# Two of a trunk's eight gate chunks issued inside the first attention steps, and one linear-attention tile per gate half

## The reference

```python
(aq, ak, av, ag, iq, ik, iw, bq, bk, bv, bg, blr) = split(rmsnorm(x) @ even_w_in)
a_out = dsa_attention(aq, ak, av, iq, ik, iw, rel_bias) * silu(ag)   # 8 heads of 64
g_out = head_rmsnorm(gla_chunked(bq, bk, bv, log_a)) * silu(bg)      # 4 heads, values of 128
mix = concatenate([a_out, g_out]) @ even_w_out
```

## Time and profile before

| | us |
|---|---|
| median of 3 runs (lowest to highest) | 1117.87 (1117.31 to 1119.39) |
| profiled execution | 1114.39 |
| its span, first to last instruction | 1112.6 |
| gate loop on PE, 16 halves | about 286 to 422 |
| the search on DVE | about 163 to 432 |
| first pair's steps 0 to 7 | 435 to 512 |
| mean granted clock of PE (1 is 2.4 GHz) | 0.961 |

### The profile page before, as it was taken

The page is one execution under the profiler, slowest core; times in us unless marked ns, Lnnn a source line. Parts: engine busy times, 40 slices in busy tenths (PEclk is TensorE's granted clock), DMA queues, the critical chain, the costliest instruction groups (busy, mean ns, idle before and its releaser), DMA issues.

```text
span 1112.6 us, 14632 instructions
## 1 busy us (share of the span) xinstructions
PE 1011.4 (91%) x5642; PEld 815.4 (73%) x5642; DVE 689.8 (62%) x1220; ACT 458.0 (41%) x780; POOL 268.1 (24%) x199
## 2 busy tenths in 40 slices
PE   4996889989999999789999778989999999895997
PEld 3885679968877776557777566878788888684885
DVE  5314679997779597874554462574539393967042
ACT  6323552253422323335555563433246363573031
POOL 2210212102332322313131564120313122124000
PEclk8998999989999999899999898999999999997999
DMA  7251102101112223101010434322211121112052
GB/s 242 63 71 38 39 1 77 39 1 38 57 56 87 76 67 114 40 25 43 16 53 24 156 106 154 111 75 76 81 52 57 38 57 39 38 38 92 22 189 75
DMA packets 71738, 75.81 MB, mean 68 GB/s; under 512 B 5064, under 2 KB 58360, under 8 KB 71672
## 3 DMA queue, kind: packets, MB, share of 16 engines
q1 hardware_dynamic: 70400, 73.30, 21.1%
q10 hardware_dynamic: 1272, 1.62, 1.3%
HBM read 58.13 MB, written 16.25 MB: 67 GB/s over the span
## 4 chain that ended last, share of the span: by engine, by line
PE 76%; DVE 13%; ACT 5%; issue 4%; POOL 1%; DMA 1%; DVEq 0%; SPq 0%; POOLq 0%; ACTq 0%
PE ps L1588 21%; PE ps L1590 20%; PE ps L1589 20%; PE ps L1833 2%; PE ps L1817 2%; PE ps L1676 2%; PE ps L1768 1%; DVE prob L1370 1%; PE ps L1678 1%; PE ps L1765 1%; PE ps L1677 1%; ACT relu L861 1%; DVE ysL L1525 1%; PE ps L1736 1%; DVE y L1517 1%
## 5 line engine op out<-in xcount | busy, mean ns | idle before, releaser
L1588 PE MATMUL ps<-hH,wH 128*128 128x512 f32 x384 | 159.1, 414 | 15.5 <-DVE qkL L1358 10.0
L1228 DVE TENSOR_SCALAR_CACHE_REDUCE junk<-score,cand 128x384 bf16<-128x384 f32 (+2 forms) x192 | 169.7, 942 | 1.3
L1590 PE MATMUL ps<-hH,wL 128*128 128x512 f32 x384 | 152.7, 398 | 0.0
L1589 PE MATMUL ps<-hL,wH 128*128 128x512 f32 x384 | 152.3, 397 | 0.0
L612 POOL TENSOR_TENSOR wL<-raw,wH 128x1024 fp32r<-128x1024 f32 x32 | 77.1, 2413 | 157.3 <-ACT wH L768 157.3
L1588 PE MATMUL ps<-h1H,w_slot_H 128*128 128x512 f32 x256 | 100.4, 392 | 2.5 <-DVE h1L L1472 2.5
L1590 PE MATMUL ps<-h1H,w_slot_L 128*128 128x512 f32 x256 | 100.3, 392 | 0.0
L1589 PE MATMUL ps<-h1L,w_slot_H 128*128 128x512 f32 x256 | 100.2, 391 | 0.0
L1588 PEld LDWEIGHTS ps<-hH,wH 128*128 128x128 f32 x384 | 73.6, 192 | 35.3 <-issue 21.3
L1590 PEld LDWEIGHTS ps<-hH,wL 128*128 128x128 f32 x384 | 73.6, 192 | 16.2
L1589 PEld LDWEIGHTS ps<-hL,wH 128*128 128x128 f32 x384 | 73.9, 192 | 13.3
(11 more groups left out here) (242 smaller groups left out, 2266.7 us busy)
## 6 DMA issues: line engine op xcount, KB each, us to landing
raw<-in_even_w_in SPq DMA_DIRECT2D x32, 512.0 KB, 4.0
xt<-in_x SPq DMA_DIRECT2D x16, 512.0 KB, 5.6
raw<-in_odd_w_in SPq DMA_DIRECT2D x16, 512.0 KB, 3.9
gate_d<-gst SPq DMA_DIRECT2D x16, 256.0 KB, 2.2
raw_row<-in_even_w_out SPq DMA_DIRECT2D x8, 512.0 KB, 3.4
x_d<-xt SPq DMA_DIRECT2D x8, 512.0 KB, 2.6
raw_row<-in_odd_w_out SPq DMA_DIRECT2D x8, 512.0 KB, 3.2
xt<-x_d SPq DMA_DIRECT2D x8, 512.0 KB, 4.7
```

Of the source, the lines that this page charges most:

```text
L1228: return steps(dve.tensor_scalar(junk1[:, j % 3, 0:(qb + 1) * P], score_of(qb), threshold, None, op, ALU.add, accum_out=dst[:, j:j + 1]))
L1588: pe.matmul(dst, lH, rH, start=k == 0, stop=False)
L1589: pe.matmul(dst, lH, rL, start=False, stop=False)
L1590: return pe.matmul(dst, lL, rH, start=False, stop=k == nk - 1)
```

## The change

- Chunks 22 and 23 become pair 0's query and key; `bg`'s last two gate chunks become 24 and 25 (`C_LATE`). The gate loop has 12 halves in place of 16.
- The four late gate halves are units among the fillers, behind (0, 2) and (0, 3). `FILLERS` has six parts in each of steps 0 to 3 and four in steps 4 to 7 (before: 4, 4, 2, 2, 2, 2, 4, 4). The first six units go round over banks 3, 5 and 0, and PE waits for the bank's last user. Banks 3 and 5 are also used by the logits from step 4 on, so `head_logits(4)` waits until the gate halves are copied.
- ACT evicts a late gate half (`late_gate`: copy, wait for POOL's last product, sigmoid) at the start of the step behind the one in which it ends; POOL multiplies it behind `near_bias` and `near_first`; SP stores it. `high` and `low` of each chunk from 24 on stand a step behind the last unit of the chunk two before.
- `gla_at` puts one tile in each half: turn, update, output of tile t at halves `8t//7 + 1`, `+2`, `+3` (before `7t//4 + 1`, `+2`, `+4`). DVE's `gla_step(t)` stands at pass `35 + 5t//2` (before `34 + 3t`). The store of a tile is issued one half behind its output.

```diff
...
-    C_AV, C_BV, C_BQK, C_AG, C_BG, C_PAIR, C_WOE, C_ODD, C_WOO = 4, 8, 12, 16, 20, 24, 32, 40, 56
+    C_AV, C_BV, C_BQK, C_AG, C_BG, C_PAIR, C_LATE, C_WOE, C_ODD, C_WOO = 4, 8, 12, 16, 20, 22, 24, 32, 40, 56
+    EARLY_G = C_PAIR - C_AG
...
-    PRODUCTS += [("pair", p, f) for p in range(PAIRS) for f in range(4)]
+    PRODUCTS += [("pair", 0, f) for f in range(2)]
+    UNITS = [("pair", 0, 2), ("pair", 0, 3)]
+    UNITS += [("g", c, hf) for c in (C_LATE, C_LATE + 1) for hf in range(2)]
+    UNITS += [("pair", p, f) for p in range(1, PAIRS) for f in range(4)]
+    PRODUCTS += UNITS
...
-        turned = 7 * t // 4 + 1
-        return turned, turned + 1, min(turned + 3, 15)
+        turned = 8 * t // 7 + 1
+        return turned, turned + 1, turned + 2
...
+    def unit_bank(unit):
+
+        if unit in UNITS[:6]:
+            return (3, 5, 0)[UNITS.index(unit) % 3]
+        return 7 if unit == ("pair", 0, 1) else 0
+
+    def before_in_bank(unit):
+
+        for other in PRODUCTS[nth_product(*unit) - 1:nth_product("pair", 0, 0) - 1:-1]:
+            if unit_bank(other) == unit_bank(unit):
+                return other
...
-    parts = [(p, f, part) for p in range(PAIRS) for f in range(4) for part in range(4)][8:]
+    parts = [(unit, part) for unit in UNITS for part in range(4)]
     FILLERS, ended = [], {}
-    for a, count in enumerate([4, 4, 2, 2, 2, 2, 4, 4] + [2] * 16):
+    for a, count in enumerate([6] * 4 + [4] * 4 + [2] * 16):
         FILLERS.append(parts[:count])
-        for p, f, part in parts[:count]:
-            ended[p, f] = a
+        for unit, part in parts[:count]:
+            ended[unit] = a
...
+        for t in range(NT):
+            if gla_at(t)[2] + 1 >= 2 * EARLY_G:
+                store_gla(t)
...
+        def store_late_gate(n, hf):
+            sp.wait_ge(silu_done, 2 * (EARLY_G + n) + hf + 1)
+            sp.dma_start(gate_d[EARLY_G + n, :, hf * HALF:(hf + 1) * HALF], gst_late[:, hf, :]).then_inc(gate_out[hf], 16)
...
-        load_raw(C_PAIR + 3)
+        load_raw(C_LATE + 1)
...
+        for n in range(2):
+            load_raw(pair_chunk(1, n))
+            for hf in range(2):
+                store_late_gate(n, hf)
+        load_raw(pair_chunk(2, 0))
+        load_raw(pair_chunk(2, 1))
...
-        for i in range(KD):
+        for i in range(EARLY_G):
...
+            for n in range(2):
+                for hf in range(2):
+                    if a == ended["g", C_LATE + n, hf] + 1:
+                        pool.wait_ge(proj_copied, copy_count("g", C_LATE + n, hf))
+                        pool.tensor_tensor(gst_late[:, hf, :], gst_late[:, hf, :], g_sig_late[:, :], ALU.mult).then_inc(silu_done, 1)
+            for c in range(C_LATE, C_WOE):
+                if a == ended[last_unit(c - 2)] + 1:
+                    low(c)
...
+        def late_gate(n, hf):
+
+            act.wait_ge(proj_full, nth_product("g", C_LATE + n, hf) + 1)
+            if n:
+                act.wait_ge(gate_out[hf], 16 * (EARLY_G + n))
+            bank = unit_bank(("g", C_LATE + n, hf))
+            act.activation(gst_late[:, hf, :], ps[:, bank, :], ACT.Copy)
+            act.wait_ge(silu_done, 2 * (EARLY_G + n) + hf)
+            act.activation(g_sig_late[:, :], ps[:, bank, :], ACT.Sigmoid).then_inc(proj_copied, 1)
...
-            for p, f in ended:
-                if ended[p, f] == a - 1:
-                    split_pair(p, f)
+            for kind, x, f in UNITS:
+                if ended[kind, x, f] == a - 1:
+                    if kind == "pair":
+                        split_pair(x, f)
+                    else:
+                        late_gate(x - C_LATE, f)
...
+            for c in range(C_LATE, C_WOE):
+                if a == ended[last_unit(c - 2)] + 1:
+                    high(c)
...
-                if n == 34 + 3 * t:
+                if n == 35 + 5 * t // 2:
...
+            kind, x, f = unit
+            hf, j = divmod(f, 2) if kind == "pair" else (f, x % 2)
             if part == 0:
-                pe.wait_ge(w_lo, C_PAIR + 2 * p + j + 1)
-                if (p, f) == (0, 0):
+                pe.wait_ge(w_lo, (pair_chunk(x, j) if kind == "pair" else x) + 1)
+                before = before_in_bank(unit)
+                if unit == ("pair", 0, 0):
                     pe.wait_ge(proj_copied, copy_count("g", C_PAIR - 1, 1))
-                elif (p, f) == (0, 1):
+                elif unit == ("pair", 0, 1):
                     pe.wait_ge(st_ready, NCH - 2)
-                else:
-                    pe.wait_ge(proj_free, low_count("pair", p, f) - 1)
-            last = weights_first(PAIR_BANK(p, f), (wH[:, j], wL[:, j]), hf, ks=range(2 * part, 2 * part + 2))
+                elif before is not None and before[0] == "pair":
+                    pe.wait_ge(proj_free, low_count(*before))
+                elif before is not None:
+                    pe.wait_ge(proj_copied, copy_count(*before))
...
+            if n == NT // 2:
+                pe.wait_ge(proj_copied, copy_count("g", C_LATE + 1, 0))
...
```

More of the change, by code:

```diff
@@ L296, in last_product, with last_unit, pair_chunk @@
             return nth_product("bqk", BQK_ORDER[c - C_BQK], 1)
[L297 to L299 removed]
+        return nth_product(*last_unit(c))
+    def last_unit(c):
+        if c < C_PAIR or C_LATE <= c < C_LATE + 2:
+            return ("g", c, 1)
+        return ("pair", 0 if c < C_LATE else (c - C_LATE) // 2, 2 + c % 2)
+    def pair_chunk(p, j):
+        return (C_LATE + 2 * p if p else C_PAIR) + j
     def before_in_slot(c):
@@ L484, in _ @@
                 sp.dma_start(gate_d[c - C_AG, :, hf * HALF:(hf + 1) * HALF], gst[:, hf, :]).then_inc(gate_out[hf], 16)
-                if hf == 0 and c >= C_AG + 3:
-                    store_gla(c - C_AG - 3)
+                for t in range(NT):
+                    if 2 * (c - C_AG) + hf == gla_at(t)[2] + 1:
+                        store_gla(t)
             load_raw(c + 3)
-        for t in range(5, NT):
-            store_gla(t)
+        for t in range(NT):
+            if gla_at(t)[2] + 1 >= 2 * EARLY_G:
+                store_gla(t)
+        def store_late_gate(n, hf):
+            sp.wait_ge(silu_done, 2 * (EARLY_G + n) + hf + 1)
+            sp.dma_start(gate_d[EARLY_G + n, :, hf * HALF:(hf + 1) * HALF], gst_late[:, hf, :]).then_inc(gate_out[hf], 16)
         def load_near(p):
@@ L711, in _ @@
                     scale_gla(2 * (a - 26) + t)
-            for p in range(1, PAIRS):
-                for j in range(2):
-                    if a == ended[p - 1, 2 + j] + 1:
-                        low(C_PAIR + 2 * p + j)
+            for n in range(2):
+                for hf in range(2):
+                    if a == ended["g", C_LATE + n, hf] + 1:
[4 more added lines that the diff above has]
+                    low(c)
             if 25 <= a < 33:
@@ L936, in gla_result @@
             ins.then_inc(o_out, 1)
-        for i in range(16):
+        for i in range(2 * EARLY_G):
             c, hf = C_AG + i // 2, i % 2
@@ L998, in _ @@
                     exponent(a, i)
-            for p in range(1, PAIRS):
-                for j in range(2):
-                    if a == ended[p - 1, 2 + j] + 1:
-                        high(C_PAIR + 2 * p + j)
+            for c in range(C_LATE, C_WOE):
+                if a == ended[last_unit(c - 2)] + 1:
+                    high(c)
             if a == 30:
@@ L1413, in _ @@
                 for hf in range(2):
+                    dve.wait_ge(gate_out[hf], 16 * EARLY_G)
+            if a == NT + 2:
+                for hf in range(2):
                     dve.wait_ge(gate_out[hf], 16 * KD)
@@ L1420, in _ @@
                 gate_b(pieces_at(a - 1)[1])
-            for p, f in ended:
-                if ended[p, f] == a - 1:
+            for kind, p, f in UNITS:
+                if kind == "pair" and ended[kind, p, f] == a - 1:
                     low_pair_result(p, f)
@@ L1850, in _ @@
             for part in range(4):
-                pair_part(0, f, part)
+                unit_part(("pair", 0, f), part)
         pe.wait_ge(o_out, NT)
@@ L1860, in _ @@
                 if parts:
-                    pair_part(*parts.pop(0))
+                    unit_part(*parts.pop(0))
                 if i == 0:
@@ L1867, in _ @@
             for part in parts:
-                pair_part(*part)
+                unit_part(*part)
             if pieces_at(a)[1] is not None:
```

26 lines of the change are left out of this document (14 added, 12 removed).

## The result

| | before | after |
|---|---|---|
| median, us (lowest to highest, runs) | 1117.59 (1116.26 to 1119.39, 4) | 1147.16 (1145.75 to 1148.70, 4) |
| ratio to before (95% interval) | | 1.0271 [1.0253, 1.0289] |
| profiled execution, its span | 1114.39, 1112.6 | 1145.75, 1144.0 |
| mean granted clock of PE | 0.961 | 0.942 |

The change makes the kernel 2.7% slower: 29.6 us by the medians, 31.4 by the spans. The forecast was 23.5.

The account below looks back on a forecast made before the run. It took the PE-DVE hand-over of tiles, not PE's load, to set the gate loop's length. First logits 8.5 us later plus steps 15.0 us longer gave 23.5, so 1141 us, range 1124 to 1153.

Parts of the forecast that it names:

- rival (3): Gate loop: the clock stays low through the alternating tiles, up to 23 us in five tiles; 1155 us; chance 12%.
- alternation in the loop: Gate loop: PE and DVE wait for each other in turn for tiles 1 to 5; search ends 7.7 us later.
- low clock in the loop: Gate loop: PE's five pauses slow the matmuls behind them, 0.5 us a tile, 2.5 in all; bounds nothing to 14.
- shorter hand-over: From search end to first logits: 1.3 us in place of 2.97, as DVE no longer waits for the second unit.
- steps 0 to 7, without low clock: First pair's attention steps: more PE work and new waits, 87.9 us against 72.9 by the same arithmetic, 15.0 longer.
- low clock in the steps, beyond before's 4.1: Steps 0 to 7: the 4.1 us of low clock in before carried over unchanged, giving 92.0 against 77.0.
- upper bound, +20: Steps 0 to 7: 20 us longer if PE's idle 7 us before step 0 put it at the low clock.
- Rival (2): Steps 0 to 7: masks cover the extra work, only the loop costs, 8.5 plus 0 to 3; 1128 us; chance 12%.
- Rival (1): Gate loop: PE sets the pace, DVE's `att` copy being there at each next turn; 21.8 us less; 1110; chance 9%.
- The table loads: Steps 2 and 4: ACT's late sigmoid needs a 1.28 us load, the next exponential another; no added drain counted.
- step 4's wait for POOL's product: Step 4: the late gate waits for POOL's product, which stands behind `near_bias`; PE waits 3.5 us.
- DVE's collisions with POOL: Steps 1 to 4: POOL's conversions beside mask making cost DVE 2.1 us each, nothing while PE is late; uncovered up to 8.

Follow-up runs that it names:

- experiment 2: The changed kernel with useless matmuls filling PE's five pauses ahead of the attention products of tiles 2 to 6; 1137.53 us, 1.0182.
- experiment 9: The changed kernel with 40 useless matmuls in PE's 9.48 us pause ahead of the first logits; 1144.58 us, 1.0252.
- experiment 1: The changed kernel with PE's tile stages in each gate half ordered output, update, turn in place of turn, update, output; 1120.89 us, 1.0040.
- experiment 4: The changed kernel with the four late gate halves' sigmoid computed as an exponential, so no function table is switched; 1147.91 us, 1.0278.
- experiment 8: On top of experiment 1, POOL's product of a late gate half moved ahead of `near_bias`; 1122.23 us, 1.0051.
- experiment 6: On top of experiment 5, `high` and `low` of chunk 24 ahead of step 0, fillers respread to 6, then 4 a step; 1113.86 us, 0.9972.
- experiment 5: On top of experiment 1, the six filler parts of step 0 issued ahead of the first logits; 1116.82 us, 1.0008.

## Why the prediction was right, and which terms were mis-sized

The forecast was slower by 23.5 us, 1141; it is 29.6, 1147.16, inside the range and nearly midway to rival (3) at 1155. The spans, term by term (31.4 in all):

| term | forecast | measured | from |
|---|---|---|---|
| alternation in the loop | +7.7 | +7.5 | experiment 2 |
| low clock in the loop | +2.5 | +10.1 | after against experiment 2 |
| shorter hand-over | -1.7 | -1.5 | 1.64 us for 3.18, `need` to first logits |
| ahead of the loop | 0 | -2.2 | first turn at 294.76 for 296.98 |
| steps 0 to 7, without low clock (87.9 for 72.9) | +15.0 | some +15 | see below |
| low clock in the steps, beyond before's 4.1 | 0 | some +4 | experiment 9, step 1, step 4 |
| behind step 8 | 0 | -1.4 | 599.4 for 600.8 us |

**The mechanism was right.** PE and DVE hand each tile to and fro, and the search ends later with fewer halves beside it. Experiment 1 shows that it is the order, by taking the alternation away with all halves where they were. Stepping both streams gave 7.7 us; the chip gave 7.5.

**The low clock in the loop was mis-sized by four.** The step that failed was "I take 0.5 a tile": it gave each pause about what one pause in before's steps had cost. In after the low level lasts for three stretches of 13.65 us in the loop, where before has none there. And what runs in them right behind the pause is turn, update and output, which DVE waits for: some 4 us more in each of three tiles and nothing in the other two (experiment 2), not 0.5 in each of five. The upper bound of that term, 14, was for 1.5 times the time in every tile; 10.1 lies near it. Rival (3), 1155, had the right mechanism and was too large: it is 14 us above the forecast, where the result is 6. The argument against it, matmuls between the pauses, was no protection. It also shows in the pauses: the five took 3.3, 3.6, 0.8, 5.1 and 0.7 us, 13.4 in all where 18.5 was forecast, as slower gate halves used up the rest.

**The steps.** Steps 2, 3, 5, 6 and 7 came within 0.5 us of the working without low clock, and step 0 too where the clock was held up (8.9, experiment 9). The excess over that working is 8.15 us: 2.5 in step 0, shown to be the clock; 1.65 in step 1 and 3.0 in step 4 (granted clock of that step 0.78), which I put down to it as well, but from the rows alone; and 1.0 in small sums. For step 4 two other traces speak too: in experiments 4 and 9 its wait is as long but its granted clock is 0.88, and it lasts 14.6 us in place of 15.4. To carry over before's 4.1 us was the mistake; 8.15 is about twice that. The forecast had the case in its upper bound, +20 with the pause ahead of step 0; the steps are at +19.1. `wL` of chunk 24 came 6.73 us after step 1's start (forecast 6.8), and PE's waits were 2.28, 1.16 and 3.95 us (2.7, 1.5, 3.5).

**Some of the closeness is luck.** The two clock terms were some 12 us too small together. The -2.2 ahead of the loop and the -1.4 behind step 8, neither of them forecast, took 3.6 of that away.

**Rival (2), the steps' work covered:** false, +19.1. **Rival (1), PE paces the loop:** false for this order. But its condition is what experiment 1 brings about, and there the loop gains 8.7 us, not 21.8: PE has time to spare then (its pause of 9.48 us), and the search with 12.7 us of waits left sets the end.

**The table loads.** The forecast had the loads themselves in steps 2 and 4. Leaving them out gave 1.0 us in step 2 and nothing in PE's wait of step 4 (experiment 4), and changes the ratio by 0.0007, inside both intervals. The drain was left at nothing, and rightly. The Trainium skill ("ScalarE: Activation LUTs", "What ACT_TABLE_LOAD costs") adds some 1.38 us of drain to a switch. The trace does not agree: the sigmoid starts 1.29 us behind the load's start, and from the gate's copy to ACT's next copy it is 2.39 us in after and 1.09 without the switch, 1.30 in all. **Half right:** step 4's wait for POOL's product. It is there with its size, but experiment 8 shows that without it the masks take its place, so that of the 3.95 us it costs under 2 (steps 4 and 5 together, 25.3 for 23.6). The forecast's sum by steps could not show that, since it went from PE's waits and not from what is late behind them. And DVE's collisions with POOL, taken as hidden under PE, are so in after: DVE is busy 63.46 us in the steps where it was 55.17, and PE waits nowhere for a mask.

```profile
448.50:544.60 96.10, 88.24 (x487) 66.49 (x487) 63.46 (x112) 41.11 (x76) 31.88 (x31) 0.92 0.15 42
```

Experiment 6 shows them again as soon as PE is earlier.

The -2.2 ahead of the loop and -1.4 behind step 8 are within the scatter of single executions, as far as the traces show. The first turn starts at 294.76 and 294.83 in after and experiment 9 and at 296.30 in experiment 4, with the same instructions ahead of it. Behind step 8, experiments 1 and 4 have 599.2 and 601.5 us, with the same work there. What makes this scatter is open.

## What to carry to other kernels

Before taking work off the fuller engine, step both streams through the hand-overs: where each instruction in a cycle waits for the other engine's last, that cycle sets the time, and freed time becomes pauses. In such a cycle, what the other engine waits for goes first and what waits for it goes last; here this one line was worth 26 of 30 us, while in the kernel before, where it put one awaited stage behind another, it cost 4. A pause of TensorE ahead of a short chain that somebody waits for cost more here than its own length, through the clock: filling pauses with useless matmuls is a cheap way to measure how much, and moving real work into them (experiments 5 and 6) is what turned the change into a small gain. But work that is taken out of a step can open new pauses there, and then the low clock only moves on (experiment 5).

## What the runs showed of the hardware

Five pauses of PE of 0.7 to 5.1 us, 16 to 21 us apart, left the granted clock at 0.81 over 90 us (0.98 with them filled, 1.00 in experiment 1, where one of 1.6 us is left), though PE was busy 88% of that time. The three of 3.3, 3.6 and 5.1 us each have a stretch of 13.65 us at the lower level with them, the two of 0.8 and 0.7 none. But pauses of 1.2 and 1.7 us close behind one another had one of 17.1 us (experiment 5). The small matmuls of 64 rows suffered as the large ones: an output of 3.10 us took 5.2. One pause of 9.5 us cost 2.5 us in the next 11.

Single DVE operations beside a POOL conversion of a weight took 1.5 to 2.1 us longer, the small ones as the large: a mask operation of 896 columns 3.08 us for 1.15 (experiment 6), a settling operation 2.28 for 0.17 before; `need` took 1.68 for 0.17 (experiment 6). POOL's conversion beside the mask took 3.93 us, where the mean in before is 2.41.
